# Two-block network at batch 1: first modulation by feature groups, entering decays by DMA, sums of squares in their own bank

## The reference, cut to what matters

```
mod_l = silu(c) @ mod_w[layer] + mod_b[layer]          # and the same with c_ctx: two vectors
sh1, sc1, g1, sh2, sc2, g2 = split(mod, 6)             # 1024 values each
h = rmsnorm(x, norm_mix_g[layer]) * (1 + sc1) + sh1    # shift and scale per feature
z = h @ even_w_in[0]                                   # 31 blocks of 128 output features
```

```
w = exp(seg) * cb[..., None] * dt[:, None]
y = einsum(w, x) + exp(cum)[..., None] * einsum(c, state)      # exp(cum): the entering decay
```

## Time and profile before

| | us |
|---|---|
| median of three executions | 1820.94 |
| profiled execution, its own time | 1821.2 |
| its span, first to last instruction | 1819.5 |
| PE busy | 1720.2 |
| DVE busy | 1346.0 |
| ACT busy | 847.7 |

### The profile page before, as it was taken

How to read it: one execution, slowest core, us unless ns; L and a number is a source line. 1 busy time by engine, 2 the same in 40 slices (tenths; PEclk the granted TensorE clock), 3 DMA queues, 4 the chain that set the end, 5 groups by cost and what they waited for, 6 DMA issues and landing times. The chain is left out here.

```text
span 1819.5 us, 26567 instructions
## 1 busy us (share of the span) xinstructions
PE 1720.2 (95%) x10286; PEld 1468.6 (81%) x10286; DVE 1346.0 (74%) x2523; ACT 847.7 (47%) x1476; POOL 55.0 (3%) x113
## 2 busy tenths in 40 slices
PE   4899999888999999999999998999998999999997
PEld 3788877676787888877788776988898888999997
DVE  6677874765999999967974577688975445765594
ACT  2623334735544552245553455433344467665541
POOL 0910000000000000000000000000000000000000
PEclk9999999999999999999999999999999999999998
DMA  8343432032222235743553101555455454444442
GB/s 313 119 146 111 137 117 70 1 111 74 93 93 93 94 100 197 245 152 116 165 172 117 46 1 56 200 164 155 156 185 188 134 168 139 140 128 128 151 158 86
DMA packets 65462, 237.45 MB, mean 131 GB/s; under 512 B 7423, under 2 KB 8888, under 8 KB 65080
## 3 DMA queue, kind: packets, MB, share of 16 engines
q1 hardware_dynamic: 63416, 233.13, 39.3%
q10 hardware_dynamic: 1920, 2.63, 0.5%
HBM read 234.41 MB, written 1.05 MB: 129 GB/s over the span
## 5 line engine op out<-in xcount | busy, mean ns | idle before, releaser
L460 PE MATMUL banks<-m,weights_high 128*128 128x256 f32 (+1 forms) x4336 | 1043.7, 334 | 32.0 <-DVE weights_low L496 25.4
L460 PEld LDWEIGHTS banks<-m,weights_high 128*128 128x128 f32 x4336 | 735.8, 191 | 123.4 <-issue 23.7
L460 PE MATMUL banks<-m,weights_low 128*128 128x256 f32 (+1 forms) x2168 | 713.6, 329 | 0.0
L496 DVE TENSOR_TENSOR weights_low<-weight_ring,weights_high 128x1024 fp32r<-128x1024 f32 x293 | 355.5, 1222 | 229.0 <-ACT weights_high L491 228.2
L460 PEld LDWEIGHTS banks<-m,weights_low 128*128 128x128 f32 x2168 | 414.4, 191 | 38.6
L491 ACT ACTIVATE weights_high<-weight_ring 128x1024 fp32r<-128x1024 f32 x293 | 309.1, 1057 | 245.3 <-PE banks L460 167.0
L628 DVE SCALAR_TENSOR_TENSOR m<-m,columns 128x189 f32<-128x189 f32 (+4 forms) x856 | 321.8, 452 | 24.6 <-ACT m L568 24.4
L767 DVE SCALAR_TENSOR_TENSOR m<-weight_ring,m 128x1024 bf16<-128x1024 f32 x184 | 225.1, 1224 | 18.7 <-DMA weight_ring<-in_weights 12.9
L567 ACT ACTIVATE m<-banks,columns 128x512 f32<-128x512 f32 (+1 forms) x120 | 83.2, 694 | 305.8 <-PE banks L460 305.8
L460 PE MATMUL banks<-m,weight_ring 128*128 128x256 f32 x704 | 152.1, 379 | 0.0
L460 PEld LDWEIGHTS banks<-m,weight_ring 128*128 128x128 f32 x704 | 133.7, 190 | 18.1
(11 more groups left out here) (383 smaller groups left out, 1637.2 us busy)
## 6 DMA issues: line engine op xcount, KB each, us to landing
weight_ring<-in_weights SPq DMA_DIRECT2D x433, 512.0 KB, 3.6
x<-in_tokens SPq DMA_DIRECT2D x1, 2048.0 KB, 14.7
m<-in_cmp_w SPq DMA_DIRECT2D x1, 2048.0 KB, 7.4
m<-in_cond SPq DMA_DIRECT2D x2, 512.0 KB, 5.5
out<-x ACTq DMA_DIRECT2D x8, 128.0 KB, 2.0
columns<-in_columns SPq DMA_DIRECT2D x1, 633.0 KB
m<-in_rg_w ACTq DMA_DIRECT2D x1, 512.0 KB, 3.4
m<-in_spatial_w ACTq DMA_DIRECT2D x1, 512.0 KB
```

The lines of the kernel that those rows point to most:

```text
L460: mm = pe.matmul(out, lhsT, rhs, start=p.start and i == 0, stop=p.stop and i == len(passes) - 1)
L496: dve.tensor_tensor(w_lo[:, g % PARTS, :], K.ring[:, PLACE[PRODUCT_BLOCKS[g]] % RING, :], w_hi[:, g % PARTS, :].bitcast(F32), ALU.subtract ...
```

## The change

The change has three parts.

First, only the first EARLY = 3 shift blocks (TensorE) and scale blocks (DVE) are summed in `setup`. The tokens are issued after the second weight block, the squares have four buffers. The other ten blocks follow the first three product blocks in the stream and are summed inside `even_projection`: for k = 3 to 7 the shift on TensorE, and the scale on DVE for k = 3, 5, 7 and on TensorE for k = 4, 6. TensorE calls `prepare.tensor(pe, k)` ahead of its wait for group k, and this sums the blocks of group k+1. DVE calls `modulate(k+2)` behind the low part of group k. `fill` falls from 24 to 12.

Second, the entering decays are stored to DRAM by ACT in the stage before; in the latent stage SP reads two rows for each pair, spread to all partitions, into four buffers. `enter` and its waits go, `scale` reads the buffer, and `read` needs a wait for `scaled` of the same pair.

Third, the sums of squares of the latent stage use the freed bank (TOTAL) in place of SIDE, with other waits.

```
+SHIFT_BLOCKS, SCALE_BLOCKS = range(0, KD), range(KD, 2 * KD)
+EARLY = 3
+SCALE_PE = (4, 6)
+MOD_PE = list(SHIFT_BLOCKS) + [KD + k for k in SCALE_PE]
-STREAM = spread_among(blocks_of("mod0")[:MOD_PE], blocks_of("mod0")[MOD_PE:MOD_FIRST]) + blocks_of("even_in")[:TOGETHER] \
+STREAM = [k + side for k in range(EARLY) for side in (0, KD)] + blocks_of("even_in")[:TOGETHER] \
+    + [k + side for k in range(EARLY, KD) for side in (0, KD)] \
     + spread_among(blocks_of("mod0")[MOD_FIRST:MOD_EVEN], blocks_of("even_in")[TOGETHER:]) \
...
                         if prepare and j == 0 and e * len(it.products) + k < prepare.n:
+                            prepare.tensor(pe, k)
                             pe.wait_ge(*prepare.ready.at(e * len(it.products) + k + 1))
...
+class NormaliseFirst(Normalise):
...
+    def tensor(self, pe, k):
+        if EARLY <= k + 1 < KD:
+            for b in self.on_tensor[k + 1]:
+                self.modulator.sum(pe, b, self.sums(k + 1, b))
+
+    def scalar(self, act):
+        K = self.K
+        for k in range(KD):
+            act.wait_ge(*self.scaled.at(max(k + 1, EARLY)))
+            act.wait_ge(*self.normed.at(k + 1))
+            for a, b, which in REGIONS:
+                part = self.place[k][:, a:b]
+                ins = act.activation(part, part, ACT.Identity, bias=K.mod[:, 0, k, which:which + 1],
+                                     scale=self.amp[:, which, k:k + 1])
+            ins.then_inc(*self.whole.up())
+            act.wait_ge(*self.whole.at(k + 1))
+            act.activation(self.parts[k][0], self.place[k], ACT.Copy).then_inc(*self.high.up())
...
+    def modulate(self, dve, k):
+        K, link = self.K, Link(dve, self.vector_step)
+        if k in SCALE_PE:
+            dve.wait_ge(K.mod_summed.sem, self.modulator.sum_index[KD + k])
+            link(self.modulator.take_sums(dve, KD + k, 1, self.sums(k, KD + k)))
+        else:
+            self.modulator.block(dve, PLACE[KD + k], KD + k)
+            dve.wait_ge(*K.mod_done.now())
+            m = K.mod[:, 0, KD + k, :]
+            link(dve.tensor_scalar(m, m, K.col("mod_b0", KD + k), None, ALU.add))
+            dve.wait_ge(K.mod_summed.sem, self.modulator.sum_index[k])
+        self.modulator.take_sums(dve, k, 1, self.sums(k, k))
+        self.gains(dve, k, k + 1).then_inc(*self.scaled.up())
+
+    def vector(self, dve):
+        for k in range(KD):
+            if k + EARLY < KD:
+                self.norm(dve, k + EARLY)
+            hi, lo = self.parts[k]
+            dve.wait_ge(*self.high.at(k + 1))
+            dve.tensor_tensor(lo, self.place[k], hi.bitcast(F32), ALU.subtract).then_inc(*self.ready.up())
+            if EARLY <= k + 2 < KD:
+                self.modulate(dve, k + 2)
...
         @block.sync
         def _(sync):
             modulator.load(sync)
+            load_weights(K, sync, 2 - RING)
+            sync.dma_start(K.x[:], K.dram["tokens"]).then_inc(*tokens.up(16))
+            load_weights(K, sync, 0)
             sync.dma_start(K.cols[:], K.dram["columns"]).then_inc(*loads.up(16))
             sync.dma_start(a2[0:49, :], K.dram["gla_a2"]).then_inc(*loads.up(16))
-            load_weights(K, sync, 0)
-            sync.dma_start(K.x[:], K.dram["tokens"]).then_inc(*tokens.up(16))
-            load_weights(K, sync, MOD_FIRST)
+            load_weights(K, sync, 2 * EARLY)
...
         @block.tensor
         def _(pe):
-            for b in on_tensor[:SQUARES_AT]:
-                modulator.sum(pe, b)
-            pe.wait_ge(*ones.at(1))
-            for k in range(KD):
-                sums.add(pe, k)
-            for b in on_tensor[SQUARES_AT:]:
-                modulator.sum(pe, b)
+            for k, b in enumerate(on_tensor):
+                modulator.sum(pe, b, K.bank[:, 0, 2 * k:2 * k + 2])
+                if k == 0:
+                    pe.wait_ge(*ones.at(1))
+                    for i in range(KD):
+                        sums.add(pe, i)
...
-                 Normalise(K, 0, "mix_g0", (0, 0, 8), rows, rstd=f["lf"]), gla, banks=4, acc_slots=4, fill=24, tail=12)
+                 NormaliseFirst(K, modulator, "mix_g0", rows, f["lf"]), gla, banks=4, acc_slots=4, fill=12, tail=12)
...
         act.activation(self.source, self.source, ACT.Ln).then_inc(*self.decayed.up())
+        act.wait_ge(*self.decayed.at(1))
+        act.dma_start(K.dram["entering"], self.enter).then_inc(*K.entering_stored.up(16))
...
-        for row, src in zip(self.rows, (latent, self.enter)):
-            link(dve.tensor_copy(row[0:64, :], src))
-            dve.tensor_tensor(row[64:P, :], src, row[0:64, :].bitcast(F32), ALU.subtract)
+        link(dve.tensor_copy(self.rows[0:64, :], latent))
+        dve.tensor_tensor(self.rows[64:P, :], latent, self.rows[0:64, :].bitcast(F32), ALU.subtract)
...
-                if g >= 3:
-                    pe.wait_ge(*logged.at(g - 2))
...
             def total(g):
-                pe.wait_ge(*kept.at(min(2 * g + 4, 2 * SG)))
+                if g:
+                    pe.wait_ge(*logged.at(g))
                 pe.wait_ge(*squared.at(4 * g + 4))
...
-                if i + 1 < n_pairs:
-                    enter(i + 1)
-                else:
-                    pe.wait_ge(*scaled.at(i + 1))
...
+                pe.wait_ge(*scaled.at(i + 1))
                 for e in range(2):
                     pe.matmul(outs[e], state[:, g, d, mine[e]], read[:, i % 2, e, :], start=(d == 0), stop=False)
...
+        @block.sync
+        def _(sync):
+            sync.wait_ge(*K.entering_stored.now())
+            for i, (g, q, d) in enumerate(pairs):
+                r = 32 * d + 8 * g + 2 * q
+                if i >= NE:
+                    sync.wait_ge(*scaled.at(i - NE + 1))
+                sync.dma_start(entering[:, i % NE, :, :],
+                               K.dram["entering"][r:r + 2].partition_broadcast(P)).then_inc(*landed[i % NE].up(16))
...
-                dve.wait_ge(*enters.at(i + 1))
+                dve.wait_ge(*landed[i % NE].at(16 * (i // NE + 1)))
```

More of the change, by code:

```diff
@@ L768, in block, with take_sums @@
                                      ALU.mult, ALU.mult, accum_out=K.mod[:, layer, j, c:c + 1]).then_inc(*K.mod_done.up())
[L770 to L776, removed]
+    def take_sums(self, dve, j, n, sums):
+        m = self.K.mod[:, 0, j:j + n, :]
+        return dve.tensor_tensor(m, sums.rearrange("p (j c) -> p j c", c=2), last(self.K.col("mod_b0", j, n), 2), ALU.add)
     def end(self, dve, blocks):
@@ L941, in vector, with __init__, take, sums @@
             dve.tensor_tensor(lo, self.place[k], hi.bitcast(F32), ALU.subtract).then_inc(*self.ready.up())
+class NormaliseFirst(Normalise):
+    def __init__(self, K, modulator, gain, rows, rstd):
+        Normalise.__init__(self, K, 0, gain, (0, 0, KD), rows, rstd)
+        self.modulator = modulator
+    def take(self, rows):
+        Normalise.take(self, rows)
+        self.on_tensor = [[k] + ([KD + k] if k in SCALE_PE else []) for k in range(KD)]
+        self.modulator.plan_tensor([b for k in range(EARLY, KD) for b in self.on_tensor[k]])
+        self.modulator.plan([KD + k for k in range(EARLY, KD) if k not in SCALE_PE])
+        (self.vector_step,) = self.K.counts(1)
+    def sums(self, k, b):
+        at = 2 if b >= KD else 0
+        return self.K.bank[:, 4 + k % 4, at:at + 2]
+    def tensor(self, pe, k):
+        if EARLY <= k + 1 < KD:
+            for b in self.on_tensor[k + 1]:
+                self.modulator.sum(pe, b, self.sums(k + 1, b))
+    def scalar(self, act):
+        K = self.K
+        for k in range(KD):
[8 more added lines that the diff above has]
+            act.activation(self.parts[k][0], self.place[k], ACT.Copy).then_inc(*self.high.up())
+    def gains(self, dve, a, b):
+        K = self.K
+        for which in range(2):
+            ins = dve.scalar_tensor_tensor(self.amp[:, which, a:b], K.mod[:, 0, KD + a:KD + b, which], 1.0,
+                                           K.col(self.gain, a, b - a), ALU.add, ALU.mult)
+        return ins
+    def vector_first(self, dve):
+        self.gains(dve, 0, EARLY).then_inc(*self.scaled.up(EARLY))
+        for k in range(EARLY):
+            self.norm(dve, k)
+    def modulate(self, dve, k):
[20 more added lines that the diff above has]
+                self.modulate(dve, k + 2)
@@ L954, in __init__ @@
         if not first:
-            self.place([K.take(T - t0) for _ in range(3 if beside else 2)])
+            self.place([K.take(T - t0) for _ in range(3 if beside else 5)])
     def place(self, rows):
-        self.sq, self.acc = rows[0:2], rows[-1]
+        self.sq, self.acc = rows[:-1], rows[-1]
+        self.n_sq = len(self.sq)
     def borrow(self, rows, finished):
@@ L1043, in take, with tensor @@
         self.made, self.high, self.ready = self.K.counts(3)
+    def tensor(self, pe, k):
+        pass
     def scalar_first(self, act):
@@ L2296, in spread @@
                           stop=True).then_inc(*spreads.up())
-            def enter(i):
```

(14 more changed lines are left out.)

61 lines of the change are left out of this document (32 added, 29 removed).

## The result

Eight executions of the changed kernel took 1824.55 to 1836.89 us, median 1830.87; eight of the kernel before, taken beside them, have a median of 1820.35. The ratio is 1.0065 with a 95% interval of 1.005 to 1.0079: slower by 10.5 us. The forecast was 1836, with a range of 1827 to 1845 for its own mechanism. The profiled execution is the fastest of the eight, 1824.55 us with a span of 1822.4, so its stages add up to less than +10.5.

A forecast was written before the change was run, and what follows sets the result against it. It took TensorE to bound the projection and latent stage, but not the setup, where DVE sums twelve blocks. 1821.2 + 23 (first product blocks ending later, setup gain included) - 8 (latent stage) = 1836.2, forecast 1836, own range 1827 to 1845.

The forecast's parts named there:

- Setup: Stage before the projection: tokens land earlier, fewer blocks are summed, next stage starts at 30.9 us; gain 14.3 us.
- The lock: Projection, k = 2 to 6: TensorE's and DVE's lists form one chain of products, block sums and DVE work; phase 62 us.
- a DVE leg: Projection, each group: take and gains 0.5, norm 0.71, low part 0.72, in all 1.9 us that TensorE's products wait for.
- The clock: Projection's three first product blocks: TensorE's clock six tenths of the way from full to half, 62 us between 46 and 72.5.
- Rival B: Projection: half clock throughout, the three product blocks end at 103, total 1847 us; chance 0.10.
- Latent stage: Dropping `enter` saves 0.33 us a pair, 10.5 for 32, less DVE lateness at `add`: -8 us, bounds -4 and -11.5.
- The start: Start of the latent stage: `scale(0)` no longer waits behind the turns, about 1 us gained.
- rival D: Latent stage: rows of entering decays arrive too late, each pair keeps 2.6 us or more, -8 falls away, 1844; chance 0.05.
- the signs: Expected observations, among them projection start at 31 +- 2, last early pass near 93, latent pairs about 73 us instead of 81.9.
- the phase of the three blocks: Projection's three first product blocks: 62 us from the stage's start, ending at 92.9 against 69.8, +23 us.
- Rival A: Projection: the clock stays full, +7 - 8, total 1820 us, no change; chance 0.12.
- rival C: Projection: the lists don't lock, block sums fill TensorE's waiting time, blocks end at 67.5, total 1807 us; chance 0.14.

The follow-up runs named there:

- `sums_ahead`: The changed kernel with TensorE summing the blocks of group k+2, not k+1, ahead of its products of k; 1821.24 us, ratio 0.9991 to the kernel before.
- -9.0 alone: The kernel before with only the latent stage's two parts (entering decays by DMA, sums of squares in bank TOTAL); 1811.83 us, ratio 0.9952.
- +19.3 measured alone: The kernel before with only the first part (shift and scale summed group by group, tokens early, four square buffers); 1840.13 us, ratio 1.0116.
- `early_six`: The changed kernel with EARLY = 6 and no scale block on TensorE behind the setup; 1825.42 us, ratio 1.0022 to the kernel before.

## Why the prediction was right

**Setup.** Predicted 30.9 for the next stage's start (its terms add up to 30.7), 29.8 in the profile. Tokens 14.3 against 15.2 forecast, sums of squares 8.55 us against 9.4; from the end of the last block sum to the stage's start it is 1.4 us (28.42 to 29.80) against 0.6. In the other runs with this setup, 30.8 to 32.1, the squares took their 9.3 to 10.1, and the missing 0.8 shows.

**The lock.** It was the mechanism forecast: products, block sums, a DVE leg, in turn, for k = 2 to 6. Three of its terms were off, and not all in one direction. The waits for the leg were 1.74, 1.89, 1.78, 1.18 and 1.06 us, 7.6 in place of 5 x 1.9 = 9.5: from k = 5 on DVE has no norm left to make. The seven sums took 1.84 + 3.86 + 2.30 + 3.75 + 3.41 = 15.2 us in place of 12.7 + 0.6 x 12.2 = 20.0. The products took the rest, 27.0 against 25.1. In all 56.8 us against 62, so +16.8 at this point, not +23.

**The clock.** Half for six tenths of the phase was right on the mean, and that is luck in part, for it isn't spread as I laid it: the clock is half in the wide passes and often full in the sums behind them, a stretch late. The products went 10.4 us of the 14.2 from full to half, the sums only 2.5 of 12.2, so the sums came out 5 us too dear. The reason I gave, bursts against waits, needs a correction from `sums_ahead`: without waits the clock is 0.76. Rival B, half clock throughout, falls: two groups read above took 3.5 and 4.0 us, as at half clock, but the sums behind them ran largely at full, and the phase ended at 86.6, far from 103. The Trainium skill, "TensorE: Matmul & The Clock Gate", HAM oscillation, puts such slow bursts down to the waits between them, where these are longer than the bursts. The prediction got to 103 by it only by counting the block sums among the waits. They are matmuls: from each first pass to the end of the sums TensorE works 6.3 to 7.5 us on end, between waits of 1.1 to 1.9, and the clock falls all the same. `sums_ahead` has no waits behind the first pass, so here the waits do not explain the slow bursts.

**Latent stage.** -7.6 in the profile and -9.0 alone, for -8. The 0.33 us of `enter` went to 0.16 a pair (2.64 to 2.48). From first pair to last TensorE's busy time fell by 8.3 us (81.1 to 72.7) in place of 10.2, and its idle time rose from 0.8 to 4.3: 2.5 of it are waits for `weigh` and 1.5 for ACT's exponentials, which the prediction did not name. The start gave 2.6 where I had 1, in part by the clock, 0.87 there before and 1.00 now. The entering rows were never waited for, which puts rival D out. Among the signs I had put 73 us from first pair to last, which does not go with my own -8: with 1 us at the start, 81.9 - 7 = 74.9. It is 77.0, 2.1 more, and the better start made up 1.6 of it. `scale` takes 684 ns from SBUF as against 686 from PSUM. The smaller fixed cost that the Trainium skill, "VectorE: DVE Perf Modes", the section on the TRN2 errata, gives for SBUF sources does not show.

**The size.** Forecast +15.6, measured +10.5. The mis-sized term is the phase of the three blocks: +16.8 in the profile and +19.3 measured alone where I had +23. Rival A (full clock) falls by the 0.70, rival C by the waits in front of each group; `sums_ahead` is what C would have needed, and even that only breaks even with the kernel before, since TensorE then bounds the whole phase, its seven sums and the low clock with them.

Open: why the later stretches of equal instructions differ by some 5 us between executions. The granted clock differs with them, but what sets its phase was not tried; it may be what makes the changed kernel's executions spread over 12 us and `sums_ahead`'s over 15, against 5 to 8 for the kernel before.

## What to carry to other kernels

Work moved out of a stage in which TensorE mostly waits, over a barrier into a stage that TensorE bounds, costs its full price there, and if two engines' program orders each hold the other's next step, the price of the waits on top. Before moving narrow matmuls (here two moving columns behind a full weight load) between wide ones, count what they do to the clock of the wide ones: here the products took 27.0 us in place of 16.6, while the sums took 15.2 in place of 12.7. In a long run of them count the narrow ones at half clock too (five sums in 14.6 us in `early_six`). A replication by matmul that an idle DMA queue can do is worth moving even when the next engine is close behind: 0.33 us less a pair gave 0.16 at once.

## What the runs showed of the hardware

TensorE's clock fell with TensorE never idle: in `sums_ahead` the mean was 0.76 from 42.62 to 77.66, where it was busy for 35.03 of 35.04 us and alternated 2 to 6 us of wide passes with block sums. Two levels show in the rows: nine 512-column passes take 2.1 us at a granted clock of 1.00 (2.4 GHz) and 4.0 at 0.50 (1.2 GHz; 55.31 to 59.32), a block sum 1.84 and 3.41. The granted clock answers late: it was full in the window from 50.0 of sums alone, behind one of wide passes, and half in the next of wide passes.
